# Two blocks of a hybrid network on one core: reordered waits in three stages, and VectorE instead of GpSimd for the additions to x

## The reference

```python
# first block
h = rms_norm(x, g[0]); hy_u, na_qkv, sc_u, gate_pre = split(h @ w_in)
y_a = hyena_mixer(hy_u, ...)            # twice: y = irfft(rfft(z) * kf), with a gate
y_b = neighbourhood_attention(q, k, v)  # 8 heads of 64, 16x8 windows
y_c = short_conv_mixer(...)
x = x + rms_norm(merged @ w_out, g[1])                    # passage r1, then h = norm n2
x = x + rms_norm(memory_cross_attention(h, mem_n), g[3])  # passage r3, then h = norm n4
x = x + rms_norm(conv_glu_ffn(h), g[5])                   # passage r5, then h = norm n6
# second block, with meta tokens in front
c_q, c_kv, k_rope, ... = split(rms_norm_2(h) @ w_in_2)
q  = rms_norm_2(c_q) @ w_qb             # latents
kv = rms_norm_2(c_kv) @ w_kvb           # keys k_nope and values v
```

## Time and profile before

| | us |
|---|---|
| median of 3 runs | 1816.38 |
| lowest and highest | 1814.66, 1820.78 |
| the profiled execution, whole | 1813.58 |
| its span, first to last instruction | 1811.5 |
| TensorE busy | 1749.2 (97% of the span) |
| VectorE busy | 1231.0 (68%) |
| ScalarE busy | 824.6 (46%) |
| GpSimd busy | 343.4 (19%) |
| mean granted TensorE clock | 0.988 |

### The profile page before, as it was taken

The page is one execution under the profiler, slowest core; times in us unless marked ns, Lnnn a source line. Parts: engine busy times, 40 slices in busy tenths (PEclk is TensorE's granted clock), DMA queues, the critical chain, the costliest instruction groups (busy, mean ns, idle before and its releaser), DMA issues.

```text
span 1811.5 us, 25518 instructions
## 1 busy us (share of the span) xinstructions
PE 1749.2 (97%) x10101; PEld 1465.9 (81%) x10101; DVE 1231.0 (68%) x1973; ACT 824.6 (46%) x1436; POOL 343.4 (19%) x292
## 2 busy tenths in 40 slices
PE   8999999999999999989999999898989999999998
PEld 6778777789998878768888888797756789999788
DVE  6878855579885367355777742466466669887996
ACT  5433344454444444343444432345458645555333
POOL 2013501021101130141111110150010123332302
PEclk9999999999999999999999999999998999999999
DMA  5222322236554321222333232232230155775753
GB/s 199 93 84 91 105 90 81 74 100 160 154 141 164 127 93 61 91 70 90 97 94 93 93 105 94 82 119 69 79 104 22 59 155 147 194 182 139 208 130 100
DMA packets 64950, 200.71 MB, mean 111 GB/s; under 512 B 7674, under 2 KB 10362, under 8 KB 64704
## 3 DMA queue, kind: packets, MB, share of 16 engines
q1 hardware_dynamic: 49824, 164.08, 28.1%
q0 software_dynamic: 14432, 34.48, 8.8%
q10 hardware_dynamic: 576, 0.52, 0.1%
HBM read 192.77 MB, written 6.29 MB: 110 GB/s over the span
## 4 chain that ended last, share of the span: by engine, by line
PE 81%; DVE 9%; issue 3%; ACT 3%; POOL 2%; DMA 0%; SPq 0%; DVEq 0%; POOLq 0%; ACTq 0%
PE ps L439 25%; PE ps L441 25%; PE ps L440 24%; PE ps L444 3%; PE ps L3938 1%; DVE ws_l L375 1%; POOL sums L487 1%; ACT ws_h L367 1%; PE ps L3955 1%; POOL x L1897 1%; DVE fb_l L2983 1%; PE ps L1142 0%; DVE mg_l L952 0%; DVE h_l L618 0%; DMA raw<-in_w_hy 0%
## 5 line engine op out<-in xcount | busy, mean ns | idle before, releaser
L375 DVE TENSOR_TENSOR ws_l<-raw,ws_h 128x1024 fp32r<-128x1024 f32 x216 | 302.1, 1404 | 250.3 <-ACT ws_h L367 249.9
L439 PE MATMUL ps<-h_h,ws_h 128*128 128x512 f32 (+2 forms) x1140 | 445.3, 391 | 20.1 <-DVE h_l L618 8.2
L440 PE MATMUL ps<-h_l,ws_h 128*128 128x512 f32 (+2 forms) x1140 | 433.7, 380 | 0.0
L441 PE MATMUL ps<-h_h,ws_l 128*128 128x512 f32 (+2 forms) x1140 | 433.1, 380 | 0.0
L367 ACT ACTIVATE ws_h<-raw 128x1024 fp32r<-128x1024 f32 x216 | 226.2, 1052 | 227.3 <-PE ps L441 223.5
L439 PEld LDWEIGHTS ps<-h_h,ws_h 128*128 128x128 f32 x1140 | 217.1, 190 | 77.9 <-issue 17.1
L441 PEld LDWEIGHTS ps<-h_h,ws_l 128*128 128x128 f32 x1140 | 217.2, 191 | 42.4
L440 PEld LDWEIGHTS ps<-h_l,ws_h 128*128 128x128 f32 x1140 | 217.7, 191 | 38.5
L439 PE MATMUL ps<-fb_h,ws_h 128*128 128x256 f32 x572 | 160.9, 281 | 1.4 <-DVE tmp L3117 1.4
L441 PE MATMUL ps<-fb_h,ws_l 128*128 128x256 f32 x572 | 160.8, 281 | 0.0
L440 PE MATMUL ps<-fb_l,ws_h 128*128 128x256 f32 x572 | 160.1, 280 | 0.0
(11 more groups left out here) (561 smaller groups left out, 3578.4 us busy)
## 6 DMA issues: line engine op xcount, KB each, us to landing
raw<-in_ffn_up SPq DMA_DIRECT2D x88, 512.0 KB, 3.6
raw<-in_w_merge SPq DMA_DIRECT2D x36, 512.0 KB, 4.1
raw<-in_ffn_down SPq DMA_DIRECT2D x22, 512.0 KB, 3.5
raw<-in_w_down SPq DMA_DIRECT2D x22, 512.0 KB, 4.6
raw<-in_w_hy SPq DMA_DIRECT2D x12, 512.0 KB, 4.0
raw<-in_w_sc SPq DMA_DIRECT2D x12, 512.0 KB, 3.5
s<-in_ffn_up SPq DMA_DIRECT2D x17, 256.0 KB, 4.3
s<-in_ffn_up POOLq DMA_DIRECT2D x17, 256.0 KB, 5.2
```

Of the source, the lines that this page charges most:

```text
L375: dve.e.tensor_tensor(w.lo, raw[n % NRAW][:], w.hi, ALU.subtract).then_inc(*lo_made.says(("lo", n)))
L439: pe.e.matmul(o, a.hi, b.hi, start=start, stop=False, skip_group_check=True)
L440: pe.e.matmul(o, a.hi, b.lo, start=False, stop=False, skip_group_check=True)
L441: return pe.e.matmul(o, a.lo, b.hi, start=False, stop=stop, skip_group_check=True)
```

## The change

1. In hyena's way back TensorE takes the slices as 0, 2, 1, 3.
2. In local attention the rings of banks are others: scores 0 and 7, projections 5 and 6, transposes 1 and 2, outputs 3 and 4; the transposes of the values go over 1 to 4.
3. In latents ScalarE reads `wv` out ahead of the high part of the second half of `ckv`.
4. In latents the value products 0 to 2 stand behind the keys of p = 0, on TensorE and on ScalarE alike; 3 and 4 stay behind p = 1.
5. In the three passages VectorE makes the additions to x for m = 2 to 7 as well, each behind the low part of tile m - 1; GpSimd is left with the sums of squares.

```diff
@@ I(o)
-                for i in range(4):
+                for i in (0, 2, 1, 3):
                     pe.wait_ge(("KY", o, 4 * q + i))
@@ na_pe
-        bs, b1, bT, bO = Ring(place, (0, 1)), Ring(place, (2, 3)), Ring(place, (4, 5)), Ring(place, (6, 7))
+        bs, b1, bT, bO = Ring(place, (0, 7)), Ring(place, (5, 6)), Ring(place, (1, 2)), Ring(place, (3, 4))
-            ring = Ring(place, (4, 5, 6, 7))
+            ring = Ring(place, (1, 2, 3, 4))
@@ residual_dve
-            if m == 1:
-                h_rest(nv, 0, ngain, dst(0))
-                dve.wait_ge(("rs", v, 1), ("x", "again", 1) if again else None)
-                dve.e.tensor_tensor(x[:, 1, :], x[:, 1, :], T[i][:, 0:L], ALU.add).then_inc(
-                    *dve_part.says(("x", v, 1), ("gone", ("rs", v, 1))))
-            elif m == 2:
-                h_rest(nv, 1, ngain, dst(1))
-            elif m > 3:
-                h_rest(nv, m - 2, ngain, dst(m - 2))
+            if m:
+                h_rest(nv, m - 1, ngain, dst(m - 1))
+                dve.wait_ge(("rs", v, m), ("x", "again", m) if again else None)
+                dve.e.tensor_tensor(x[:, m, :], x[:, m, :], T[i][:, 0:L], ALU.add).then_inc(
+                    *dve_part.says(("x", v, m), ("gone", ("rs", v, m))))
             beside(m)
-        h_rest(nv, 6, ngain, dst(6))
         h_rest(nv, 7, ngain, dst(7))
@@ residual_pool
-        for m in range(2, 8):
-            pool.wait_ge(("rs", v, m), ("x", "again", m) if again else None)
-            pool.e.tensor_tensor(x[:, m, :], x[:, m, :], t_slot(("rs", v, m))[:, 0:L], ALU.add).then_inc(
-                *pool_part.says(("x", v, m), ("gone", ("rs", v, m))))
         squares_pool(nv)
@@ latent_pe, with VALUES_BEHIND = (0, 1, 2), (3, 4); inside the loop over p, behind the keys
+            for i in VALUES_BEHIND[p]:
+                a, m = FIVE[i]
@@ latent_act, behind root(("kv", 1), ...)
+            for tt in range(5 if m else 0):
             act.wait_ge(("ckv g", m))
             act.e.activation(ckv[:, HALVES[m]].hi, crx[2][:, HALVES[m]], ACT.Copy).then_inc(*act_part.says(("ckv hi", m)))
-        for tt in range(5):
```

More of the change, by code:

```diff
@@ L3299, in program @@
     FIVE = [(16 + 128 * i, 128) for i in range(4)] + [(0, 16)]
+    VALUES_BEHIND = (0, 1, 2), (3, 4)
     park_in = [signal(f"x_parked{m}") for m in range(8)]
@@ L3365, in latent_pe @@
                 key_part(p, i, bank(("kn", p, i), main), ws(n)[:, 128 * p:128 * p + 128])
[L3366 to L3369, removed]
+            for i in VALUES_BEHIND[p]:
+                a, m = FIVE[i]
+                pe.wait_ge("KW hi" if i == 4 else None, "KW lo" if i == 4 else None)
+                mm(bank(("vl", i), main)[0:m, 0:384], ckv[:, a:a + m], ws(n)[:, 512:896], True,
+                   True).then_inc(*products.says(("done", ("vl", i)), over(n) if i == 4 else None))
     def key_part(p, i, o, w):
@@ L3461, in latent_act @@
             root(("kv", m), 264, 128, kv_roots[m])
+            for tt in range(5 if m else 0):
+                n = 128 if tt < 4 else 16
+                act.wait_ge(("done", ("wv", 3)), ("token scale", "n6"))
+                act.e.activation(V2[0:n, tt, :], out_of(("wv", tt))[0:n, 0:384], ACT.Copy,
+                                 scale=rt("n6")[:, tt:tt + 1] if tt < 4 else 1.0).then_inc(
+                    *act_out.says(("V2 made", tt), ("free", ("wv", tt))))
             act.wait_ge(("ckv g", m))
             act.e.activation(ckv[:, HALVES[m]].hi, crx[2][:, HALVES[m]], ACT.Copy).then_inc(*act_part.says(("ckv hi", m)))
-        for tt in range(5):
[L3465 to L3469, removed]
         fd, fs, fq = Follow(chunk_act), Follow(chunk_act), Follow(chunk_act)
@@ L3485, in latent_act @@
                 key_hi(p, i)
[L3486 to L3490, removed]
+            for i in VALUES_BEHIND[p]:
+                m = 128 if i < 4 else 16
+                act.wait_ge(("done", ("vl", i)))
+                act.e.activation(V[0:m, i, :], out_of(("vl", i))[0:m, 0:384], ACT.Copy).then_inc(
+                    *act_out.says(("V made2", i), ("free", ("vl", i))))
         act.wait_ge("lam sums")
```

## The result

| | before | the change |
|---|---|---|
| median of 4 runs, us | 1816.25 | 1830.57 |
| lowest and highest | 1814.66, 1820.78 | 1828.62, 1832.13 |
| the profiled execution's span | 1811.5 | 1827.9 |
| TensorE waiting for `h_rest` (L618) | 8.2 | 17.0 |
| mean granted clock | 0.988 | 0.984 |

The change makes the kernel slower: the ratio is 1.0073, 95% interval 1.0048 to 1.0099, so +8.7 to +18.0 us around +13.3 (the medians as they stand differ by 14.3). Forecast were +10.5 (1826.9) and a range to 1832; the spans of the two profiled executions differ by 16.4.

The account below looks back on a forecast made before the run. TensorE, busy 97% of the span, was taken to bound the kernel. Terms 5.5 + 5.5 + 1.8 - 1.3 - 1.0 = +10.5 on the profiled 1813.58, plus 2.8 to the median, gave 1826.9 us; range 1812 to 1832.

Parts of the forecast that it names:

- The bound of +0.2: Hyena into local attention: a loss of 0.2 us if idle time gathered in one place brings the low clock.
- the last link: Latents, before the scores: ScalarE's fewer value read-outs shorten a wait of 0.72 us; latents -1.0 in all.
- my bound of 0: Latents: no gain if VectorE's last low parts of p = 1, unmoved, hold the scores.
- The step before it: Latents: queries of p = 1 wait for the bank until VectorE has made QN_l, spending the 2.2 us earlier start.
- my list of signs: Trace signs forecast: additions about 1.9 us; in latents no QN_l wait and one under 1 us before queries of p = 1.
- 5.5 each: Passages r3 and r5: TensorE waits at every tile for low parts of h, +5.5 us per passage.
- the period's terms: Passages, per tile: GpSimd's sum waiting from 1.46, its 1.28, then 0.48 to the addition's end; 3.2 us.
- the margin: Passages: GpSimd's sum asks for the port 0.1 us before VectorE's next addition could start.
- the likeliest case: GpSimd first at the port in the passages: +10.5 us in all, 1826.9 us, chance 0.48.
- the third rival: Pauses in r1, r3, r5 or before scores bring the low clock: 1.7 to 5 us on top, chance 0.12.
- VectorE first: Passages: VectorE's addition wins the port, period 2.65 us; +4.1 in all, 1820.5 us, chance 0.24.
- The cheaper addition: Passages: sums miss VectorE's two-input instructions, period 2.14 us, -0.8 a passage; 1811.7 us, chance 0.12.

Follow-up runs that it names:

- only_latents: Parts 3 and 4 alone, against the kernel before: 1815.98 against 1816.39 us, ratio 0.9996.
- Part 3 alone: Only wv read out earlier, value products all behind p = 1, against the kernel before: 1817.78 against 1817.75 us, ratio 0.9991.
- sums_late: Part 5 alone, GpSimd's sums of squares starting only after VectorE's last addition, against the kernel before: 1815.31 against 1816.39 us, ratio 0.9984.
- both_filled: Changed kernel with nine unused products in each pause, before local attention's first scores and latents' scores, against the kernel before: 1828.31 against 1814.00 us, ratio 1.0069.
- sums_one_behind: Part 5 alone, each GpSimd sum of squares waiting for VectorE's next addition, against the kernel before: 1817.14 against 1817.75 us, ratio 0.9995.

## Why the prediction was right, and where not

**Hyena into local attention.** Right: the scores came 1.4 earlier for 1.3 forecast, held by VectorE, with 2.2 of idle time gathered before them. The bound of +0.2, with the low clock, was what the first execution then showed (+1.5 behind the scores, 0.1 net); in the second the gain stayed (-1.4). No run shows what decides between the two.

**Latents.** The size was right (-1.0 to -1.2 for -1.0), the last link was not: I had ScalarE's read-outs end the wait for the scores, and it is VectorE's KN_l, after a wait of 2.2. That low part starts where it did before, within 0.15 (1249.12 in only_latents, whose timeline is 1.65 behind there, for 1247.61), which was the condition of my bound of 0; the scores came 1.2 earlier all the same, since before they had waited that much longer, for ScalarE. That -1.0 fits is thus partly luck. The step before it was right: the queries of p = 1 wait for QN_l of p = 0 (1.1, where my list of signs had under 1, and none for QN_l) and spend the earlier start. Part 3 alone shows how much they spend: it wins 2.05.

**Passages.** Right in mechanism and size. Period 3.24 for 3.2; 5.7 and 5.6 for 5.5 each; r1 1.7 for 1.8. That GpSimd asks first, by 0.1, was the point on which it hung; the rows show 0.10. Three of the period's terms are off and cancel: the sum starts 1.36 behind the end of an addition, not 1.46, takes 1.33 for 1.28, and the addition ends 0.56 behind it for 0.48. The addition took 1.77, where my list of signs had about 1.9. That the margin decided is shown by the run that lets GpSimd ask one addition later: r3 then loses 1.7, and the median nothing.

**The sum.** The terms as measured add up to 1.7 + 5.7 + 5.6 - 1.4 - 1.1 = +10.5, as forecast; the medians differ by 14.3, and the interval, 8.7 to 18.0, holds both. What stands between them in the first pair of profiled executions is 5.9: the low clock (1.5, 1.5, 1.2 and 1.2) and a late start. Before's first execution is one of the few without the low clock behind latents; its second is 3.6 longer, after's second 3.5 shorter than its first. The step that was mis-sized is thus the last one: I took the 2.8 between before's profiled execution and its median for the changed kernel too, where it was 0.8 (1829.74 to 1830.57), and gave the low clock no share in the likeliest case. The measured 1830.57 lies where the third rival (low clock on top, 1828.6 to 1832, chance 0.12) had put it, and for one of its places, ahead of the scores, it was right in the first execution; in the passages, where it was to cost most, next to nothing was lost to it. In r5 the low clock lasted half as long again as in before (10.2 us for 6.8, from 1175 us on), and r5 cost 5.6, as it did in after's second execution, where it lasted 6.8: TensorE was waiting there anyway. What the low clock did cost came, but for the scores, behind latents and in attention, which the rival does not name; that the time fell in its range is in part luck.

**The rivals.** VectorE first did not occur. The cheaper addition did not either, but its condition is what sums_late makes: period 2.15 for 2.14. Of its -0.8 a passage there was -0.4 in r3, since the sums, then last, hold TensorE.

Open: whether the pauses of the changed kernel make the low clock more frequent over many runs. Two executions of each cannot tell that from chance, and both_filled, whose profiled execution has the clock at 1.00 at both places, has a median as far above before's as the changed kernel has (14.3 both).

## To carry to other kernels

Before moving an instruction from GpSimd to VectorE, list what GpSimd will do instead at that time: what counts is how much of its instruction is left when VectorE's next one with two SBUF inputs asks, and here a shift by one addition was the difference between 13 us and nothing that the medians can tell. A wait removed in front of a stage that another engine holds gathers as one longer pause further on (1.62 and 1.50 here became one of 2.20). Behind that pause the clock fell in two executions of three and took the gain back; filled with unused products, it did not fall in two of two, which is too few to call filling the cure, and the real work tried in its place was missed a little later. And compare two executions by the low-clock stretches first, since the same kernel differed by 3 to 4 us, most of it through them.

## What the runs showed of the hardware

VectorE waited out GpSimd's instruction to the hundredth: 0.54 less on one, 0.54 less on the other. L1871, which reads one operand from a bank, took 0.74 to 0.75 beside a sum (sums_one_behind, where the sum starts 0.15 into it) as it did with none (sums_late).

The stretches at the lower level (1.2 GHz) cost alike: summed over windows of 1 us, the granted clock falls short by about 1.7 us in each, or by two or three times that (3.4, 5.1) where they join. On TensorE's timeline that is 1.2 to 1.5. In two executions of one program some stand at the same place and some do not (before's two share those at 647, 667, 787 and 1169 us and differ from 1250 us on).

In 8 of the 13 executions beside before's first, TensorE falls 0.9 behind that one between 830 and 1055 us, by 0.12 in each 25 us, with no pause and no stretch at the low clock. No run here tells why.
